# Transposes in place of identity and flip matmuls, GpSimd's list reordered, and normalisation parts three steps apart instead of four, in a hybrid decoder layer

## The chip, the cores and the metric

The kernel runs on one core of one Trainium2 chip. The metric is device time in microseconds (us) from start to end of the program; three runs of the kernel before are shown, and their median counts. The profile is of one execution, and its times count from the first instruction. TensorE multiplies, VectorE and ScalarE work element by element, GpSimd does the same more slowly without reaching PSUM, and SyncE only issues DMAs. Each engine works its own list in order; semaphores order the engines among one another.

## The reference, cut to what matters

One layer over 2,064 prompt positions (16 of them learned meta tokens) and 8 samples, in fp32. A combined projection gives, among others, the input of a convolution branch and queries, keys and values. The kernel's middle stage computes two things:

```
# convolution branch: 31 taps per channel, bias, LayerNorm over the 512 channels
y  = depthwise_causal_conv(u, w) + b
yn = (y - mean(y)) * rsqrt(mean((y - mean(y))**2) + 1e-5)   # then scale, shift, silu in the last stage
# attention branch, 8 heads, 2 key heads: masked softmax over the selected keys
p  = softmax(q @ k.T / 8 + bias, over the selected keys);  o = p @ v
```

The last stage multiplies both branches with their gates, projects them with `w_out`, adds the input and normalises.

## The kernel before, in words

The program is four stages with a barrier between them; the third, `attend_and_convolve`, is the one that changes, and the fourth, `mix_out`, reads what it writes (`d_y`, the normalised convolution, and `d_mix`, the gated attention).

**Steps.** Positions are cut into 17 tiles of 128, the last (16) with 16 prompt rows and the samples. Tiles go from 16 down to 0; each but the last has four pairs of heads, and one pair of one tile is a step p (`pairs`, 65 steps, step 0 for tile 16; tile i has steps 4(15-i)+1 to 4(15-i)+4). A tile of index i attends to (i+1) x 128 keys, so steps become shorter. In a step TensorE issues the scores of step p+1 (`logits`, lines 1710 and 1711, into psU), waits for the exponentials of step p, transposes them in groups (line 1717, into psT) and multiplies with the values (line 1733, into psO). VectorE adds mask and bias to the scores and takes the maximum (line 1606), ScalarE takes the exponential (line 1461) and copies the transposes to SBUF (line 1436, which is a helper, `evac`, for all copies out of psT). VectorE is about one step ahead of TensorE, as its work on step p+1 needs only TensorE's first part of step p.

**R.** After the fourth pair of a tile the reciprocal sums of the softmax, spread by VectorE to `rx` (line 1585), are turned into `rb` by four matmuls with the identity (line 1807); ScalarE copies them ahead of its next exponentials, and `finish` (VectorE) multiplies them into the output two steps later and signals `tile_done`.

**The convolution** runs in steps 2 to 16 (line 1746). Its normalisation is cut into nine parts k (`NORM`): tile 16 with the samples, and then two tiles each. Three lists give the step of each part's work (`SUM_STEP`, `SQ_STEP`, `TURN_STEP`). Part k goes: VectorE sums over channels in a partition (`sums`), TensorE sums over partitions (line 1752, job M), ScalarE copies the mean; two steps later VectorE subtracts it, GpSimd squares (`squares`, line 1409); at `SQ_STEP` VectorE sums the squares, TensorE sums over partitions (job V), ScalarE copies the variance; GpSimd takes its power -1/2 (`inverse_deviation`, lines 1415 and 1416); at `TURN_STEP` VectorE multiplies it in (`normalise`), and TensorE turns the part (`turn`, lines 1757 to 1763), four matmuls a tile against a matrix `flip` that reverses each run of 32 positions. ScalarE copies the result to `cT` in channel-major order (lines 1495 to 1501), and SyncE stores it one step later (line 1350).

**GpSimd's list** goes step by step: first `band_mask` for the tile whose turn it is (every fourth step, for the tile that begins three steps later), then the convolution's work. `band_mask` waits for `tile_done` of two tiles before and for the DMA of the mask (line 1298), converts the mask (line 1387) and adds the bias band of eight heads (line 1395).

**SyncE's list** goes by the same steps: in each, the stores of turned tiles first, then the store of a finished tile's `mix` and the loads of the tile two ahead (queries, gate, mask).

**psT** has two buffers, taken in the order of a list of jobs (`ptjobs`) which follows the same step numbers; a job waits until the job two before it has been copied.

Of the kernel before, what the change touches and what calls it, by code (L numbers as in the profile page):

```python
# [19 lines left out]
P = 128  # L20
NT = -(-LP // P)
LAST = NT - 1
# [3 lines left out]
CC = C // 128  # L26
# [28 lines left out]
def t5_bucket(rel):  # L55
# [10 lines left out]
                  flip=(529 + BANDX + LS, 128), avg=(529 + BANDX + LS + 128, 128))  # L66
# [4 lines left out]
WIN = 32  # L71
WROWS = 2 * WIN
WPT = P // WIN
NWP = WPT * LAST + 1
# [1044 lines left out]
CONV_STEP = [x for q in CONV_STEPS for x in q]  # L1119

NORM = [[LAST]] + [[i - 1, i] for i in range(LAST - 1, 0, -2)]
SUM_STEP = [18 + 4 * k for k in range(len(NORM))]
SQ_STEP = [s + 3 for s in SUM_STEP]
TURN_STEP = [s + 5 for s in SUM_STEP]

# [1 line left out]
def attend_and_convolve(nc, t, mem):  # L1127
# [38 lines left out]
    with ExitStack() as ctx:  # L1166
# [6 lines left out]
        yc = sb("yc", [128, NW, P])  # L1173
# [13 lines left out]
        rx = sb("rx", [128, GRP, 2, HD])  # L1187
# [21 lines left out]
        flip = sb("flip", [128, 2, 128])  # L1209
# [151 lines left out]
        @block.gpsimd  # L1361
        def _(pool):
            G = nc.gpsimd
            G.memset(q16[:, :, :].bitcast(f32), 0.0).then_inc(q16_zero, 1)
            G.memset(uw[:, NWP:NW, :], 0.0).then_inc(uw_zero, 1)
            G.memset(mix[:, 0], 0.0).then_inc(mix_zero, 1)
            load_pages(pool, range(hp), ptab, t.cache_v, "o s n d -> (o s) (n d)", vpage, vpp_in)
            steps = [0]

            def chained(ins):  # L1370

                steps[0] += 1
                ins.then_inc(pstep, 1)
                pool.wait_ge(pstep, steps[0])
            pool.wait_ge(band_in, 16)

            def band_mask(n):

                i = TILE_ORDER[n]
                s = n % 2  # L1380
                a, k = band0(i), width(i) - band0(i)
                j0 = a - (i - 1) * P
                if n >= 2:
                    pool.wait_ge(tile_done, n - 1)
                if i >= 2:
                    pool.wait_ge(m_in[s], masks_loaded(n))
                    chained(G.tensor_scalar(mask[:, s, 0:width(i)], mask[:, s, 0:width(i)], -NEG, NEG, ALU.mult, ALU.add))  # L1387
                else:
                    chained(G.memset(mask[:, s, 0:P], 0.0))
                    chained(G.tensor_copy(mask[:, s, i * P:(i + 1) * P], part(mem.cst, "causal")))  # L1390
                if n == 0:
                    pool.wait_ge(b16_in, 16 * NH)
                    G.tensor_tensor(out=bm[:, s, 0, 0:k], in0=band16[:, :], in1=mask[:, s, a:a + k], op=ALU.add).then_inc(bm_ready, 1)
                    return
                G.tensor_tensor(out=bm[:, s, :, 0:k], in0=band[:, :, j0:j0 + k],
                                in1=mask[:, s, a:a + k].unsqueeze(1).to_broadcast([128, NH, k]), op=ALU.add).then_inc(bm_ready, 1)
            def squares(k):

                n = norm_count(k)
                pool.wait_ge(sub_done, k + 1)  # L1400
                if k == 0:
                    G.memset(cT[:, 0], 0.0).then_inc(turn_zero, 1)
                else:
                    pool.wait_ge(s2_done, k)
                if NORM[k][0] == LAST:
                    to = y2[:, 0:n, :]
                else:
                    to = y2[:, 0:n, :].rearrange("p (w i) c -> p w i c", i=2)
                G.tensor_tensor(out=to, in0=norm_windows(k, yc), in1=norm_windows(k, yc), op=ALU.mult).then_inc(y2_done, 1)

            def inverse_deviation(k):

                n = norm_count(k)
                pool.wait_ge(act_pt, act_copies(("V", k)))
                chained(G.tensor_scalar(ve[:, 0:n], var[:, k % 2, 0:n], 1.0, LN_EPS, ALU.mult, ALU.add))
                G.tensor_tensor(out=rs[:, k % 2, 0:n], in0=ve[:, 0:n], in1=mhalf[:, 0:n], op=ALU.pow).then_inc(rs_done, 1)
            chained(G.memset(mhalf[:, :], -0.5))

            mask_step = [0, 0] + [first_step(n - 1) + 1 for n in range(2, NT)]
            for p in range(NP_):  # L1420
                for n in range(NT):
                    if mask_step[n] == p:
                        band_mask(n)
                for k in range(len(NORM)):
                    if SUM_STEP[k] + 2 == p:
                        squares(k)
                    if SQ_STEP[k] + 1 == p:
                        inverse_deviation(k)

        @block.scalar  # L1430
        def _(act):
            A = nc.scalar

            def evac(job, out, src):
                act.wait_ge(pe_pt, pt_no[job] + 1)
                A.activation(out, src, ACT.Copy).then_inc(act_pt, 1)  # L1436
# [27 lines left out]
            for p, (i, j) in enumerate(pairs):  # L1464
                for b, k in groups(p):
                    job = ("T", p, b, k)
                    n = t_no[job]
                    act.wait_ge(pe_pv, NS + 1 + max(0, n - 2))
                    m = sides(p) * k * P
                    evac(job, pts[:, n % 3, 0:m], PT[:, pt_no[job] % 2, 0:m])  # L1470
                if p and j == GRP - 1:
                    n = tile_no[i]
                    if n >= 2:
                        act.wait_ge(tile_done, n - 1)
                    evac(("R", p), rb[:, n % 2].rearrange("p c t -> p (c t)"), PT[:, pt_no["R", p] % 2, :])
                if p + 1 < NP_:
                    if j == GRP - 1 and tile_no[i] >= 1:
                        act.wait_ge(ri_ready, tile_no[i])
                    exps(p + 1)
                for k, tiles in enumerate(NORM):  # L1480
                    if SUM_STEP[k] == p:
                        evac(("M", k), mean[:, k % 2, 0:norm_count(k)], PT[:, pt_no["M", k] % 2, 0:norm_count(k)])
                for k, tiles in enumerate(NORM):
                    if SQ_STEP[k] == p:
                        evac(("V", k), var[:, k % 2, 0:norm_count(k)], PT[:, pt_no["V", k] % 2, 0:norm_count(k)])
                for k, tiles in enumerate(NORM):
                    if TURN_STEP[k] == p:
                        for i in tiles:
                            n, job = turned[i], ("Y", k, i)
                            pt = PT[:, pt_no[job] % 2]  # L1490
                            if n >= 2:
                                act.wait_ge(cT_out[n % 2], 16 * (n // 2))
                            if i == LAST:
                                act.wait_ge(turn_zero, 1)
                                act.wait_ge(pe_pt, pt_no[job] + 1)
                                A.activation(cT[:, n % 2, :, SROW:SROW + NS],
                                             pt[:, P:P + NS * CC].rearrange("p (s g) -> p g s", g=CC), ACT.Copy)
                                evac(job, cT[:, n % 2, :, 0:WIN], pt[:, 0:P].rearrange("p (g o) -> p g o", o=WIN))
                            else:
                                evac(job, cT[:, n % 2].rearrange("p g (w o) -> p w g o", o=WIN),  # L1500
                                     pt.rearrange("p (w g o) -> p w g o", g=CC, o=WIN))

        @block.vector
        def _(dve):
# [137 lines left out]
        def _(pe):  # L1642
# [111 lines left out]
            def turn(k, i):  # L1754
                pt = take_pt(("Y", k, i))
                if i == LAST:
                    T.matmul(pt[:, 0:P], yc[:, NWP - 1, :], flip[:, 0, :], start=True, stop=True)
                    for s in range(NS):
                        last = T.matmul(pt[:, P + s * CC:P + (s + 1) * CC], yc[:, NWP + s, :],
                                        flip[:, 0, 0::WIN], start=True, stop=True)  # L1760
                else:
                    for w in range(WPT):
                        last = T.matmul(pt[:, w * P:(w + 1) * P], yc[:, w * LAST + i, :], flip[:, 0, :], start=True, stop=True)
                last.then_inc(pe_pt, 1)
            logits(0)
            pe.wait_ge(s_norm, 1)
# [20 lines left out]
            for p, (i, j) in enumerate(pairs):  # L1787
# [14 lines left out]
                if p and j == GRP - 1:  # L1802
                    n = tile_no[i]
                    pe.wait_ge(ri_ready, n + 1)
                    pt = take_pt(("R", p))
                    for jj in range(GRP):
                        last = T.matmul(pt[:, jj * P:(jj + 1) * P],
                                        rx[:, jj].rearrange("p a d -> p (a d)"), ident, start=True, stop=True)
                    last.then_inc(pe_pt, 1)
                for e, (q, a, k) in enumerate(CONV_JOBS):  # L1810
                    if CONV_STEP[e] == p:
# [408 lines left out]
```

## Time and profile before

| | us |
|---|---|
| median of three runs | 1701.25 (1700.36 to 1712.43) |
| span of the profiled execution, first to last instruction | 1700.2 |
| median less span | 1.05 |
| attention stage (880 to 1480): TensorE / ScalarE / VectorE / GpSimd busy | 543 / 333 / 290 / 110 of 600 |

The rows further down come from the profile of that execution. Matmuls overlap in the pipeline, so the duration of one is longer than the distance to the next; weight loads have rows of their own (PEld). The number in square brackets behind a row is the engine's idle time before it, with the engine and line that ended it. The granted clock is 1.00 at 2.4 GHz and 0.50 at 1.2 GHz; in a window it is the mean.

### The profile page before, as it was taken

What the parts mean: (1) busy time and instruction counts of PE and PEld (TensorE: products, weight loads), DVE (VectorE), ACT (ScalarE), POOL (GpSimd) and SP (SyncE); (2) the same over time, 40 slices, a digit from 0 to 9 for tenths busy, and PEclk for the clock granted to TensorE, in tenths of its full rate; (3) what the DMA queues carried; (4) which work ended last, traced back from release to release, by engine and by line L of the source; (5) the groups of instructions that cost most, each with busy time, mean ns of one, the idle gap of its engine ahead of it and who ended that gap; (6) DMA issues with size and microseconds to landing.
All of it is one profiled execution on the core that took longest, in us unless ns stands there. A gap on an engine that the chain in (4) does not pass through costs nothing. (4 is left out here: it accounts for less than half of the span.)

```text
span 1700.2 us, 28238 instructions
## 1 busy us (share of the span) xinstructions
PE 1513.3 (89%) x10647; PEld 1292.1 (76%) x10647; DVE 1003.3 (59%) x2123; ACT 697.9 (41%) x1238; POOL 415.0 (24%) x270
## 2 busy tenths in 40 slices
PE   5688989989998789999799999999999887569998
PEld 5686979978998769999577777776767665348886
DVE  3342998878988879888443444445455555333222
ACT  4354513253112352232225545556556654344331
POOL 2111224431115803222221001112222233043220
PEclk9999999999999999999879999999999999779999
DMA  7742365221357602224561513511111112295542
GB/s 237 219 107 50 68 92 119 67 75 54 84 161 222 157 22 72 70 75 125 163 156 36 115 37 79 113 35 34 39 45 50 58 61 77 81 231 162 173 149 93
DMA packets 183355, 172.71 MB, mean 102 GB/s; under 512 B 58956, under 2 KB 155348, under 8 KB 182700
## 3 DMA queue, kind: packets, MB, share of 16 engines
q1 hardware_dynamic: 176572, 152.91, 33.7%
q10 hardware_dynamic: 6136, 16.95, 3.4%
q8 instruction: 84, 1.38, 0.3%
q0 software_dynamic: 512, 1.05, 0.2%
q14 instruction: 51, 0.42, 0.1%
HBM read 109.35 MB, written 58.19 MB: 99 GB/s over the span
## 5 line engine op out<-in xcount | busy, mean ns | idle before, releaser
L845 PE MATMUL psum<-xh,wh 128*128 128x384 f32 (+1 forms) x1040 | 345.4, 332 | 23.1 <-ACT hst L782 11.5
L845 PE MATMUL psum<-xl,wh 128*128 128x384 f32 (+1 forms) x1040 | 341.6, 329 | 0.0
L845 PE MATMUL psum<-xh,wl 128*128 128x384 f32 (+1 forms) x1040 | 341.6, 328 | 0.0
L1436 ACT ACTIVATE pts<-psT 128x512 f32<-128x512 f32 (+1 forms) x302 | 167.1, 572 | 255.1 <-PE psT L1717 232.2
L845 PEld LDWEIGHTS psum<-xh,wh 128*128 128x128 f32 x1040 | 197.6, 190 | 26.4 <-ACT hst L782 15.2
L1606 DVE CUSTOM_DVE_ANT_0 L<-psU,mask 128x512 f32<-128x512 f32 (+3 forms) x260 | 143.5, 592 | 114.6 <-PE psU L1711 113.3
L1733 PE MATMUL psO<-pts,vs 128*64 128x128 f32 x2176 | 180.3, 287 | 27.2 <-ACT pts L1436 27.2
L845 PEld LDWEIGHTS psum<-xl,wh 128*128 128x128 f32 x1040 | 197.8, 190 | 0.0
L845 PEld LDWEIGHTS psum<-xh,wl 128*128 128x128 f32 x1040 | 197.5, 190 | 0.0
L995 DVE TENSOR_SCALAR_CACHE_REDUCE hit<-scores,T 128x1792 bf16<-128x1792 f32 (+8 forms) x120 | 184.6, 1538 | 11.7 <-issue 0.9
L693 POOL TENSOR_TENSOR wl<-uw,wh 128x1024 fp32r<-128x1024 f32 x44 | 121.5, 2762 | 276.8 <-ACT wh L730 276.8
L1717 PE MATMUL psT<-cst,L 128*128 128x128 f32 x1105 | 170.4, 283 | 14.2 <-ACT L L1461 12.1
L1733 PEld LDWEIGHTS psO<-pts,vs 128*64 128x64 f32 x2176 | 113.2, 136 | 81.6 <-ACT pts L1436 56.5
L1461 ACT ACTIVATE L<-L,nm 128x1920 f32<-128x1920 f32 (+16 forms) x129 | 154.4, 1201 | 19.3 <-DVE nm L1611 18.9
L1717 PEld LDWEIGHTS psT<-cst,L 128*128 128x128 f32 x1105 | 119.3, 141 | 49.3 <-issue 20.9
L1710 PE MATMUL psU<-keys,qt 128*128 128x512 f32 (+3 forms) x320 | 128.7, 406 | 2.2 <-DVE mx L1606 1.2
L1387 POOL TENSOR_SCALAR mask<-mask 128x2064 bf16<-128x2064 bf16 (+14 forms) x15 | 18.8, 1255 | 416.8 <-DMA mask<-d_mask 416.7
L1711 PE MATMUL psU<-iqs,qt 128*128 128x512 f32 (+3 forms) x320 | 116.0, 373 | 0.0
L2095 PE MATMUL psO<-woh,fh 128*128 128x512 f32 x272 | 85.3, 395 | 27.6 <-POOL fl L1977 27.6
L2039 DVE TENSOR_TENSOR res<-psO,xr 128x1024 f32<-128x1024 f32 x17 | 20.8, 1225 | 125.5 <-PE psO L2095 125.5
L855 PE MATMUL psum<-keys,iqs 128*128 128x512 f32 (+4 forms) x172 | 70.0, 409 | 26.8 <-ACT uw L791 20.3
L791 ACT ACTIVATE uw<-psum 128x1024 f32<-128x1024 f32 (+6 forms) x100 | 76.8, 806 | 40.7 <-DVE scores L944 25.4
(269 smaller groups left out, 2507.5 us busy)
## 6 DMA issues: line engine op xcount, KB each, us to landing
uw<-in_w_in SPq DMA_DIRECT2D x28, 512.0 KB
uw<-in_w_in SPq DMA_DIRECT2D x32, 256.0 KB
qt<-d_q SPq DMA_DIRECT2D x16, 512.0 KB, 4.0
xst<-in_x_prompt SPq DMA_DIRECT2D x15, 512.0 KB, 4.0
xr<-in_x_prompt SPq DMA_DIRECT2D x15, 512.0 KB, 4.4
out_y_prompt<-fin SPq DMA_DIRECT2D x15, 512.0 KB, 3.0
gate<-d_ga SPq DMA_DIRECT2D x17, 256.0 KB, 4.4
d_mix<-mix SPq DMA_DIRECT2D x17, 256.0 KB, 2.2
```

The source lines that it names most:

```text
L693: nc.gpsimd.tensor_tensor(out=wl[:, n % 2], in0=wst[:, n % 2], in1=wh[:, n % 2].bitcast(f32), op=ALU.subtract).then_inc(w_lo, 1)
L791: nc.scalar.activation(r[:, m % 2, 0:job[4]], u[:, 0:job[4]], ACT.Relu).then_inc(act_job, 1)
L845: last = nc.tensor.matmul(u[:, 0:k * P], a[:, w % 2, cc, :], x[:, s0:s0 + k, cc, :], start=(cc == 0 and e == 0), stop=(cc == KC - 1 and e ...
L995: V.tensor_scalar(hit[:, 0:width(i)], sc[c], at[:, c:c + 1] if len(at.shape) == 2 else at[:, c], 0.0, ALU.is_ge, ALU.add, accum_out=into[: ...
L1436: A.activation(out, src, ACT.Copy).then_inc(act_pt, 1)
L1461: A.activation(L[:, b, 0:width(i)], L[:, b, 0:width(i)], ACT.Exp, bias=nm[:, b:b + 1], accum_out=es[:, tile_no[i] % 2, j % GRP + 4 * side: ...
L1606: last = V.tensor_tensor_reduce(out=L[:, b, x0:x1], in0=u[:, x0 - a:x1 - a], in1=in1, scale=1.0, scalar=3 * NEG, op0=ALU.add, op1=ALU.max, ...
L1710: T.matmul(u[:, 0:k], q, kh[:, side, a:a + k], start=True, stop=False)
L1711: T.matmul(u[:, 0:k], q, kl[:, side, a:a + k], start=False, stop=True).then_inc(pe_u, 1)
L1717: last = T.transpose(pt[:, (side * k + e) * P:(side * k + e + 1) * P], L[:, (2 * p + side) % 4, (b + e) * P:(b + e + 1) * P], ident)
L1733: last = T.matmul(OT[64 * side:64 * side + 64, tile_no[i] % 2, j * P:(j + 1) * P], vs[0:rows, b + e, 64 * side:64 * side + 64], pts[0:rows ...
L2095: last = T.matmul(O[:, s, h * 512:(h + 1) * 512], a[:, n % FS, c, :], b[:, c, h * 512:(h + 1) * 512], start=(c == W_ORDER[0] and e == 0), ...
```

## The change

Four edits. R and the turns call the transpose, with the identity as the moving operand, in place of a matmul (with the identity for R and with `flip` for the turns; the samples' small matmuls of tile 16 stay). What `flip` reversed is now reversed in ScalarE's copy, which reads each run of 32 backwards. GpSimd's list has the convolution's work ahead of the mask in a step, and the inverse deviation ahead of the squares. And parts follow one another every three steps: `SUM_STEP` goes 18, 21, ..., 42 in place of 18, 22, ..., 50; `SQ_STEP` and `TURN_STEP` stay 3 and 5 steps behind it. So turns come at steps 23, 26, ..., 47 in place of 23, 27, ..., 55.

```
-SUM_STEP = [18 + 4 * k for k in range(len(NORM))]
+SUM_STEP = [18 + 3 * k for k in range(len(NORM))]
...
             for p in range(NP_):
+                for k in range(len(NORM)):
+                    if SQ_STEP[k] + 1 == p:
+                        inverse_deviation(k)
+                    if SUM_STEP[k] + 2 == p:
+                        squares(k)
                 for n in range(NT):
                     if mask_step[n] == p:
                         band_mask(n)
-                for k in range(len(NORM)):
-                    if SUM_STEP[k] + 2 == p:
-                        squares(k)
-                    if SQ_STEP[k] + 1 == p:
-                        inverse_deviation(k)
...
-        evac(job, cT[:, n % 2, :, 0:WIN], pt[:, 0:P].rearrange("p (g o) -> p g o", o=WIN))
+        evac(job, cT[:, n % 2, :, 0:WIN], pt[:, 0:P].rearrange("p (g o) -> p g o", o=WIN)[:, :, ::-1])
...
-             pt.rearrange("p (w g o) -> p w g o", g=CC, o=WIN))
+             pt.rearrange("p (w g o) -> p w g o", g=CC, o=WIN)[:, :, :, ::-1])
...
-                    T.matmul(pt[:, 0:P], yc[:, NWP - 1, :], flip[:, 0, :], start=True, stop=True)
+                    T.transpose(pt[:, 0:P], yc[:, NWP - 1, :], ident)
...
-                        last = T.matmul(pt[:, w * P:(w + 1) * P], yc[:, w * LAST + i, :], flip[:, 0, :], start=True, stop=True)
+                        last = T.transpose(pt[:, w * P:(w + 1) * P], yc[:, w * LAST + i, :], ident)
...
-                        last = T.matmul(pt[:, jj * P:(jj + 1) * P],
-                                        rx[:, jj].rearrange("p a d -> p (a d)"), ident, start=True, stop=True)
+                        last = T.transpose(pt[:, jj * P:(jj + 1) * P], rx[:, jj].rearrange("p a d -> p (a d)"), ident)
```

## Rows read from the trace of the kernel before

**Rows 1.** Head of the page: span of the profiled execution.
```profile
span 1700.2 us, 28238 instructions
```

**Rows 2.** Windows, attention stage: length, busy time by engine, granted clock, DMA share, GB/s.
```profile
880.00:1480.00 600.00, 543.35 (x5301) 407.73 (x5299) 289.77 (x1051) 333.34 (x601) 110.16 (x60) 0.98 0.22 59
```

**Rows 3.** Timeline of weight loads: start, length, engine, line, operation, count.
```profile
1225.30 0.90 PEld L1717 LDWEIGHTS psT<-cst,L 128*128 128x128 f32 x8
...
1241.02 1.86 PEld L1763 LDWEIGHTS psT<-flip,yc 128*128 128x128 f32 x16 [0.17 <-issue]
1242.80 0.19 PEld L1710 LDWEIGHTS psU<-keys,qt 128*128 128x128 f32 x1
...
1251.72 0.97 PEld L1807 LDWEIGHTS psT<-cst,rx 128*128 128x128 f32 x8 [0.17 <-issue]
1252.61 0.19 PEld L1710 LDWEIGHTS psU<-keys,qt 128*128 128x128 f32 x1
```

**Rows 4.** Groups, 880 to 1480: count, busy, mean ns, idle before and releaser.
```profile
L1717 PE MATMUL psT<-cst,L 128*128 128x128 f32 x1099 | 169.8, 283 | 14.2 <-ACT L L1461 12.1 <-ACT uw L1436 2.1
...
L1763 PE MATMUL psT<-flip,yc 128*128 128x128 f32 x128 | 19.7, 317 | 10.0 <-DVE yc L1507 10.0
...
L1807 PE MATMUL psT<-cst,rx 128*128 128x128 f32 x128 | 19.5, 297 | 0.0
...
L1507 DVE TENSOR_TENSOR yc<-yc,rs 128x1024 f32<-128x1024 f32 (+1 forms) x9 | 11.2, 1240 | 55.0 <-POOL rs L1416 55.0
```

**Rows 5.** Timeline of GpSimd around the deviation of part 7.
```profile
1417.62 0.51 POOL L1387 TENSOR_SCALAR mask<-mask 128x384 bf16<-128x384 bf16 x1 [13.03 <-DMA mask<-d_mask]
1418.21 4.07 POOL L1395 TENSOR_TENSOR bm<-band,mask 128x2048 f32<-128x2048 f32 x1
1422.36 0.20 POOL L1415 TENSOR_SCALAR ve<-var 128x8 f32<-128x8 f32 x1
1422.65 1.65 POOL L1416 TENSOR_TENSOR rs<-ve,mhalf 128x8 f32<-128x8 f32 x1
```

**Rows 6.** Timeline of VectorE (parts 1 and 7) and ScalarE (variance of part 7).
```profile
1231.91 1.23 DVE L1507 TENSOR_TENSOR yc<-yc,rs 128x1024 f32<-128x1024 f32 x1 [4.50 <-POOL rs L1416]
...
1424.33 1.22 DVE L1507 TENSOR_TENSOR yc<-yc,rs 128x1024 f32<-128x1024 f32 x1 [8.52 <-POOL rs L1416]
...
1413.40 0.17 ACT L1436 ACTIVATE var<-psT 128x8 f32<-128x8 f32 x1
```

**Rows 7.** Timeline of TensorE: where it stood behind VectorE's lateness, and a statistic.
```profile
1273.58 0.50 PE L1710 MATMUL psU<-keys,qt 128*128 128x512 f32 x1 [1.24 <-DVE mx L1606]
...
1347.81 1.07 PE L1717 MATMUL psT<-cst,L 128*128 128x128 f32 x8 [1.03 <-ACT uw L1436]
...
1375.80 1.07 PE L1717 MATMUL psT<-cst,L 128*128 128x128 f32 x8 [0.67 <-ACT uw L1436]
...
1399.23 3.57 PE L1763 MATMUL psT<-flip,yc 128*128 128x128 f32 x16 [2.66 <-DVE yc L1507]
...
1416.41 0.39 PE L1752 MATMUL psT<-s,flip 128*128 128x8 f32 x2
...
1425.61 3.78 PE L1763 MATMUL psT<-flip,yc 128*128 128x128 f32 x16 [5.45 <-DVE yc L1507]
...
1448.66 0.85 PE L1717 MATMUL psT<-cst,L 128*128 128x128 f32 x6 [0.40 <-ACT uw L1436]
```

**Rows 8.** Windows, TensorE's steps 46, 47, 50 and 51.
```profile
1386.85:1391.80 4.95, 4.64 (x43) 3.54 (x42) 2.21 (x14) 3.16 (x10) 0.62 (x1) 1.00 0.65 191
1391.80:1402.46 10.66, 7.69 (x57) 6.50 (x56) 4.32 (x16) 4.35 (x13) 5.94 (x3) 0.86 0.01 2
1412.99:1416.66 3.67, 3.36 (x33) 2.66 (x32) 2.27 (x11) 2.55 (x8) 0.00 (x0) 1.00 0.97 305
1416.66:1429.05 12.39, 6.63 (x47) 5.86 (x46) 4.05 (x12) 3.78 (x10) 6.84 (x5) 0.77 0.01 4
```

**Rows 9.** Timeline of SyncE's queue: the mask's DMA issue.
```profile
1413.53 0.50 SPq L1298 DMA_DIRECT2D mask<-d_mask  x1
```

**Rows 10.** Timeline of ScalarE: copies of a pair of turned tiles, and the next copy.
```profile
1242.97 1.07 ACT L1436 ACTIVATE uw<-psT 128x512 f32<-128x512 f32 x2
1246.15 1.09 ACT L1436 ACTIVATE pts<-psT 128x512 f32<-128x512 f32 x2 [2.11 <-PE psT L1717]
```

## The prediction

> **What bounds the kernel now.** I read the busy shares first, then the stretch that the change touches, then the waits inside it. The profiled execution spans 1700.2 us [rows 1]; the median of the three timed runs, 1701.25, is 1.05 us above it, so a saving worked out on this trace is taken off 1701.25. All edits lie in the attention stage, 880 to 1480 us. There TensorE has matmuls in flight for 543 of 600 us, VectorE is busy 290, ScalarE 333, GpSimd 110 [rows 2]. The next stage starts behind a barrier, so what this stage gains reaches the end one to one. A step p of TensorE is: scores of step p+1, transposes and products of step p, then the extras (R, statistics, turns). In wide tiles its order has hardly a gap; in narrow ones, from about 1340 us on, there are real stalls, and those are what I price beside the cheaper instructions.
>
> **Transposes for matmuls.** A 128x128 fp32 matmul is two load-and-multiply records here: 16 R groups of four matmuls leave 128 records, 16 turned tiles of four leave 128 [rows 4]. One R takes the weight port from 1251.72 to the next score load at 1252.61, 0.89 us; a pair of turns from 1241.02 to 1242.80, 1.78 us; eight transposes are one record each and take 0.90 us with a tail of 0.14, so (0.90 - 0.14) / 7 = 0.109 us each [rows 3]. R falls to 4 x 0.109 = 0.44 and saves 0.45, sixteen times: 7.2 us. A pair of turns falls to 0.87 and saves 0.91, eight times: 7.3, and the last tile's single matmul 0.1. Is it on the path? Behind R, ScalarE must copy R before it can do the next exponentials, and TensorE's transposes wait for those; an earlier R moves that whole chain. Behind a turn TensorE goes straight on to scores; ScalarE's two copies end 2.11 us before it gets its next tile [rows 10]. So both count in full: 14.6 us. The Trainium skill's page "TensorE: Matmul & The Clock Gate", section Terms, calls the transpose mode four times faster for fp32; that would make a transpose 0.056 us and this term 21.5 us, a time of about 1666. The row is of this very form of instruction, so I keep 0.109.
>
> **The reversal moves into ScalarE's copy,** which reads PSUM backwards inside each run of 32. No row shows a backward read. Bounds: nothing, or a doubling of 0.53 us per copy [rows 10], 8.5 us over 16 copies if none is hidden. A pair has 2.11 - 0.91 = 1.2 us of slack against 1.07, so I take nothing and keep half of the upper end, 4.3 us, for narrow tiles in the range.
>
> **GpSimd's order.** GpSimd runs one list. At a step where a mask is due it now waits for the mask's DMA, does mask and bias sum, and only then the inverse deviation. In the last full case the variance is copied at 1413.40, but GpSimd takes up the mask at 1417.62 and starts the deviation's two instructions at 1422.36 [rows 5, 6]. VectorE wants it at 1424.33 - 8.52 = 1415.81 and stands 8.52 us; in the wide tile of the other row it stands 4.50 [rows 6]. Behind it stand the next scores' evacuations, and the turn of that part, on TensorE. With the convolution's work first, the two instructions (0.20 and 1.65 us) run right behind the variance: ready at about 1415.6, just as VectorE arrives.
>
> What this wait costs on the path: TensorE stands before turns for 10.0 us in all [rows 4], of which 2.66 and 5.45 in the two worst places, and 1.24 once for score banks [rows 7]: 11.2. VectorE's lateness is felt once more in the step behind, at 1347.81, 1375.80 and 1448.66: 1.03 + 0.67 + 0.40 = 2.1 [rows 7]. And in both worst places the granted clock falls while TensorE stands: a mean of 0.86 and 0.77 in steps 47 and 51 [rows 8], so for a part of them at 1.2 rather than 2.4 GHz. Step 47 takes 10.66 us; its neighbour without a turn 4.95, with 0.25 for a statistic (1416.41 to 1416.66) [rows 7]. 10.66 - 4.95 + 0.25 - 1.78 - 2.66 = 1.5 us are the clock's. Step 51: 12.39 - 3.67 + 0.25 - 1.78 - 5.45 = 1.7. Together 3.2, and all of it goes: 16.5 us for the stalls.
>
> **Three steps apart.** Turns come at steps 23, 26, ..., 47 rather than 23, 27, ..., 55, so they leave the narrowest tiles, where VectorE had least cover. Amounts are unchanged. What now meets: (a) the mean of part k+1 and the variance of part k in one step: two copies of 0.17 us [rows 6] instead of one before the next transposes, hidden except behind R. (b) Normalise and subtract the mean in one VectorE step: 1.2 us more there; TensorE's step is longer than VectorE's list by that, so nothing. (c) R and a turn both at steps 32 and 44: the turn runs in the gap in which TensorE waits for exponentials anyway, worth up to 0.9 us each, a small gain I leave out. (d) SyncE's queue: at steps 30 and 42 the stores of a turned tile now stand ahead of the next tile's loads, and they wait for ScalarE's copies. That holds the loads 4 to 6 us; a mask is issued at 1413.53 and used at 1417.62 [rows 5, 9], so it lands 4 us after issue, and GpSimd, in order, holds the inverse deviation behind it. VectorE then stands 3 to 5 us at turns 3 and 7. Waits of that size cost between 0 and 1.24 now [rows 6, 7]; I take 1 each. (e) The mask of the tile at step 53: its bias sum ends at 1418.21 + 4.07 = 1422.28 [rows 5]. The steps ahead shrink to 3.67 - 0.25 = 3.42 us [rows 8], and VectorE could come at 1412.99 - 0.25 + 2 x 3.42 = 1419.6: the mask is up to 2.7 late. That step follows an R, where TensorE waits for ScalarE anyway; 0 to 2.7, I take 1. GpSimd's squares now ahead of the mask wait for VectorE inside the same step, shorter than the mask's DMA; the mask has two steps to spare elsewhere: nothing.
>
> **Sum:** 14.6 + 16.5 - 3 = 28 us, so 1701.25 - 28 = 1673.
>
> **Rivals.**
> A. The wait is moved, not removed: the mask ahead in GpSimd's list, or SyncE's queue, holds the deviation at most turns as now. For it: the list stays one list, and collisions (d) exist. Against: a mask falls due every 4 steps and a deviation every 3, so they can meet at one in four, and there the deviation now goes first. Then only 14.6 is left: 1687.
> B. The transposes save no time, since the path runs through ScalarE or they too take two records. Against: existing transposes are single records [rows 3]. The stalls alone, less 3: 1701.25 - 13.5 = 1688.
> C. Slower: the clock. At each of 24 places (16 R, 8 pairs of turns) matmuls become transposes; if each place sent the granted clock down once, at the 1.5 to 1.7 us of [rows 8], that is 36 to 41 us against a gain of 28: 1709 to 1714. It decides from some 19 places on. For it: both falls in [rows 8] come in narrow steps with little work on TensorE, and turns become shorter. Against: transposes are in every step of the stage, 1,099 of them, and its mean granted clock is 0.98 [rows 2, 4]. The same page, Part 4, says that the full clock does not engage for transposes. The trace so far does not bear that rule out.
>
> **Chances.** Forecast 0.72, with its own range: at best 14.6 + 16.5, the 1.8 of (c), the 0.5 of hidden statistics and no new cost, 33.4, so 1668; at worst all new costs (3, with 1.7 more for (e)), 4.3 for the copies and two new falls of the clock at 1.5, so 31.1 - 12.0 = 19.1, 1682. A 0.15, B 0.08, C 0.05. The whole range, 1666 (a transpose cheaper than its row) to 1688, takes in A and B. About 1% is what a measurement of this kernel can tell from no change, 1684.2 to 1718.3. Faster: the forecast and the lower third of A, 0.77; same: the rest of A and B and most of C, 0.20; slower 0.03, the part of C in which a fall costs more than priced.
>
> **What would show it.** R and turn records: 64 each instead of 128, at about 0.11 us. VectorE's wait for the inverse deviation: from 55.0 us over nine [rows 4] to under 20, largest at turns 3 and 7. TensorE's wait before turns: near 0, with full clock from step 23 to the last tiles. Copies of turned tiles at 0.53 us each. The stage ends near 1452 instead of 1480. I am wrong if VectorE's nine waits stay above 4 us each (A), if scores after an R start no earlier (B), or if steps with turns show a granted clock of one half (C).

## The result and the profile after

The changed kernel takes 1676.38 us (median of 4 runs, 1674.21 to 1678.09) against 1702.2 us for the kernel before (4 runs): 25.8 us saved by the medians. The ratio over all runs is 0.9834, 95% interval 0.9809 to 0.9858 (one run of the kernel before took 1712.43 us, which the median leaves aside). Timed again later, with the experiments, the ratio was 0.9852 [0.9836, 0.9867]. Forecast were 1673 us and a range of 1666 to 1688. The profiled execution spans 1676.4 us against 1700.2 [rows 1].

The saving lies in the attention stage. From its first score matmul to the next stage's first load it took 607.2 us before and takes 582.5 now, 24.7 less. The first view is the windows over it, over four of TensorE's steps (44, 52, 53 and 54), over two stretches inside them, and over the stage up to step 43 and its last 11 us: length, busy time of PE, PEld, DVE, ACT and POOL, granted clock, DMA share, GB/s.

```profile
880.00:1456.00 576.00, 526.58 (x5175) 389.75 (x5172) 298.24 (x1053) 332.01 (x601) 111.86 (x60) 0.98 0.23 62
...
1362.07:1374.65 12.58, 7.61 (x59) 6.08 (x57) 6.14 (x19) 4.29 (x11) 5.96 (x4) 0.80 0.00 1
1407.45:1412.71 5.26, 3.46 (x34) 2.74 (x33) 2.05 (x12) 1.85 (x5) 2.45 (x1) 1.00 0.00 0
1412.71:1418.23 5.52, 3.97 (x25) 2.92 (x23) 2.88 (x12) 3.84 (x11) 1.40 (x3) 0.62 0.14 50
1418.23:1422.29 4.06, 3.65 (x24) 3.07 (x23) 1.52 (x10) 1.46 (x5) 3.17 (x1) 0.68 0.65 194
...
1369.70:1376.50 6.80, 4.49 (x18) 3.91 (x19) 3.38 (x14) 3.19 (x7) 0.97 (x1) 0.50 0.00 1
1414.00:1420.80 6.80, 5.59 (x28) 4.72 (x28) 3.66 (x19) 2.90 (x10) 3.97 (x3) 0.50 0.46 145
...
880.00:1369.00 489.00, 463.06 (x4685) 342.02 (x4682) 255.12 (x844) 284.90 (x474) 91.84 (x48) 1.00 0.23 61
1444.80:1456.00 11.20, 5.31 (x24) 3.05 (x24) 3.02 (x13) 2.94 (x12) 0.00 (x0) 0.50 0.10 41
```

The stage ends at 1456, forecast 1452, and TensorE's busy time is 17 us lower than in [rows 2]. The mean clock, 0.98, hides what the single steps show: step 44 took 12.58 us at a mean of 0.80 (7.11 before), and steps 53 and 54 ran at 0.62 and 0.68 (5.52 and 4.06 us against 4.63 and 2.94 before). The next two windows are the two falls themselves: 6.8 us each at 0.50, the lower of the clock's two levels, 1.2 GHz. Up to step 43 the clock stays at 1.00; in the last 11 us it is at 0.50. The kernel before has two such stretches beside the falls of [rows 8], one right behind the turn of tile 16, at 1201, and one at its own end:

```profile
1201.60:1204.80 3.20, 3.20 (x11) 2.62 (x10) 2.75 (x10) 0.00 (x1) 0.00 (x0) 0.50 0.27 82
...
1467.80:1480.00 12.20, 6.79 (x31) 4.23 (x30) 3.66 (x16) 3.27 (x12) 0.00 (x0) 0.50 0.11 41
```

The end aside, the half clock lasts 13.7 us in either kernel: three falls of 3.4, 3.4 and 6.8 us before, two of 6.8 us now. Stalls are not gone; a few are left, in new places.

The groups of the same stretch, which answer to [rows 4]: out<-in, shape, count, then busy time, mean ns of one, and the idle time before them with what ended it.

```profile
L1717 PE MATMUL psT<-cst,L 128*128 128x128 f32 x1102 | 171.0, 284 | 8.2 <-ACT L L1461 7.8 <-ACT uw L1436 0.3
...
L1507 DVE TENSOR_TENSOR yc<-yc,rs 128x1024 f32<-128x1024 f32 (+1 forms) x9 | 12.2, 1358 | 11.3 <-POOL rs L1416 11.0
...
L1807 PE MATMUL psT<-cst,rx 128*128 128x128 f32 x64 | 11.4, 305 | 6.0 <-DVE rx L1585 6.0
...
L1763 PE MATMUL psT<-cst,yc 128*128 128x128 f32 x64 | 9.9, 298 | 0.3 <-ACT rb L1436 0.3
...
L1436 ACT ACTIVATE uw<-psT 128x512 f32<-128x512 f32 (+1 forms) x17 | 8.8, 568 | 0.0
```

R and turns are 64 records each instead of 128. VectorE's nine waits for the inverse deviation came from 55.0 us to 11.3, TensorE's waits before turns from 10.0 to 0.3. New is 6.0 us in front of R, where nothing was waited for before. The copies that now read backwards take 568 ns on average (566 before).

The weight port at a pair of turns, which answers to [rows 3] (start, length, count):

```profile
1228.72 0.86 PEld L1763 LDWEIGHTS psT<-cst,yc 128*128 128x128 f32 x8 [0.17 <-issue]
1229.54 0.19 PEld L1710 LDWEIGHTS psU<-keys,qt 128*128 128x128 f32 x1
```

1229.54 - 1228.72 = 0.82 us, where the pair took 1.78. Where VectorE still waits for the deviation, from its timeline, which answers to [rows 6]:

```profile
1182.49 1.99 DVE L1507 TENSOR_TENSOR yc<-yc,rs 128x1152 f32<-128x1152 f32 x1
1184.40 5.11 DVE L1507 TENSOR_TENSOR yc<-yc,mean 128x1024 f32<-128x1024 f32 x1
...
1276.05 1.23 DVE L1507 TENSOR_TENSOR yc<-yc,rs 128x1024 f32<-128x1024 f32 x1 [4.70 <-POOL rs L1416]
...
1366.34 1.22 DVE L1507 TENSOR_TENSOR yc<-yc,rs 128x1024 f32<-128x1024 f32 x1 [6.33 <-POOL rs L1416]
...
1409.93 0.29 DVE L1606 CUSTOM_DVE_ANT_0 L<-psU,mask 128x128 f32<-128x128 f32 x1 [3.32 <-POOL bm L1395]
```

The two waits are at parts 3 and 7, the parts of item (d). Part 7 is followed back through GpSimd's list (which answers to [rows 5]) and SyncE's queue (which answers to [rows 9]):

```profile
1183.36 5.07 POOL L1395 TENSOR_TENSOR bm<-band,mask 128x2048 f32<-128x2048 f32 x1
...
1359.38 0.73 POOL L1387 TENSOR_SCALAR mask<-mask 128x640 bf16<-128x640 bf16 x1 [14.64 <-DMA mask<-d_mask]
1360.20 4.09 POOL L1395 TENSOR_TENSOR bm<-band,mask 128x2048 f32<-128x2048 f32 x1
1364.37 0.20 POOL L1415 TENSOR_SCALAR ve<-var 128x8 f32<-128x8 f32 x1
1364.65 1.65 POOL L1416 TENSOR_TENSOR rs<-ve,mhalf 128x8 f32<-128x8 f32 x1
```

```profile
1351.62 0.91 SPq L1350 DMA_DIRECT2D d_y<-uw  x2
1352.58 0.55 SPq L1354 DMA_DIRECT2D d_mix<-mix  x1
1354.57 0.68 SPq L1298 DMA_DIRECT2D mask<-d_mask  x1
```

The mask is issued behind the turned tiles' stores, at 1354.57. GpSimd stands 14.64 us for it, does mask and bias sum, and only then the two instructions of the deviation. What that costs on TensorE (second row), with two other places that the account below comes back to:

```profile
1190.18 0.50 PE L1710 MATMUL psU<-keys,qt 128*128 128x512 f32 x1 [1.10 <-DVE mx L1606]
...
1372.02 1.12 PE L1807 MATMUL psT<-cst,rx 128*128 128x128 f32 x4 [4.50 <-DVE rx L1585]
...
1412.30 0.66 PE L1807 MATMUL psT<-cst,rx 128*128 128x128 f32 x4 [1.49 <-DVE rx L1585]
```

At 1372.02 R of step 44 stands 4.50 us for `rx`, since VectorE made it behind its 6.33 us wait; R itself then takes 1.12 us rather than 0.66 us, because the granted clock had fallen to half (from 1369.7 on). That is the form of [rows 8], in another step.

### The profile page after: what moved, and what is told of

The parts are those of the page before. It is cut to its first block and busy times, and to the rows that moved or that the text cites. A ratio compares the mean times of both kernels' runs of the same rounds, so it can differ in the third digit from the quotient of the medians.

```text
span 1676.4 us, 27980 instructions
## 1 busy us (share of the span) xinstructions
PE 1498.1 (89%) x10518; PEld 1275.7 (76%) x10518; DVE 1011.1 (60%) x2123; ACT 696.3 (42%) x1238; POOL 417.8 (25%) x270
## 3 DMA queue, kind: packets, MB, share of 16 engines
q8 instruction: 83, 1.36, 0.3%
```

## The experiments

Every ratio below is against the kernel before on the same chip.

**One edit at a time.** Each of the first three is the kernel before with one edit; the fourth is the changed kernel with two blocks of SyncE's loop exchanged.

*Transposes and reversed copy alone.* The changed kernel, with

```
-SUM_STEP = [18 + 3 * k for k in range(len(NORM))]
+SUM_STEP = [18 + 4 * k for k in range(len(NORM))]
...
+                for n in range(NT):
+                    if mask_step[n] == p:
+                        band_mask(n)
                 for k in range(len(NORM)):
-                    if SQ_STEP[k] + 1 == p:
-                        inverse_deviation(k)
                     if SUM_STEP[k] + 2 == p:
                         squares(k)
-                for n in range(NT):
-                    if mask_step[n] == p:
-                        band_mask(n)
+                    if SQ_STEP[k] + 1 == p:
+                        inverse_deviation(k)
```

> The kernel before with the transposes and the reversed copy alone (parts four steps apart, mask ahead in GpSimd's list). My theory, TensorE's issue time is on the path: 16 R at 0.45 to 0.50 us and 8 pairs of turns at 0.87 to 0.91, 14.2 to 15.3 us less than before, some 1687. Rival B, the time is hidden behind ScalarE's chain: within 3 us of before. Rival C, the clock pays for it: new windows at half clock behind R or turns, and less than 10 us gained. GpSimd and VectorE should show the same nine waits for the inverse deviation, 50 to 58 us in all.

Measured: 1698.27 us, ratio 0.9969 [0.9959, 0.9978], 5 us, where 14 to 15 were expected. VectorE's group, and TensorE's turns of parts 6 and 7:

```profile
L1507 DVE TENSOR_TENSOR yc<-yc,rs 128x1024 f32<-128x1024 f32 (+1 forms) x9 | 11.2, 1241 | 53.7 <-POOL rs L1416 53.7
```

```profile
1392.82 1.97 PE L1763 MATMUL psT<-cst,yc 128*128 128x128 f32 x8 [2.46 <-DVE yc L1507]
...
1419.79 1.97 PE L1763 MATMUL psT<-cst,yc 128*128 128x128 f32 x8 [6.49 <-DVE yc L1507]
```

VectorE waits as long as before. TensorE reaches the turn of part 7 earlier and stands 6.49 us there instead of 5.45 [rows 7]: part of what the transposes save becomes a longer stand. The fall of the clock at part 6 lasts 6.8 us instead of 3.4, and one of 3.4 us, from 1429.5, is new. In its profiled execution the stage is 10.5 us shorter; that execution, 1692.94 us, was the shortest of ten, so the median's 5 is the surer figure.

*GpSimd's order alone.* The kernel before, with

```
-                for n in range(NT):
-                    if mask_step[n] == p:
-                        band_mask(n)
                 for k in range(len(NORM)):
+                    if SQ_STEP[k] + 1 == p:
+                        inverse_deviation(k)
                     if SUM_STEP[k] + 2 == p:
                         squares(k)
-                    if SQ_STEP[k] + 1 == p:
-                        inverse_deviation(k)
+                for n in range(NT):
+                    if mask_step[n] == p:
+                        band_mask(n)
```

> The kernel before with GpSimd's new list order alone (matmuls kept, four steps apart). My theory, the mask ahead of the inverse deviation makes all nine waits: VectorE's 55 us fall to under 10, TensorE's waits before turns to near 0, both falls of the clock at 1399 and 1423 us go; 14 to 16.5 us less than before, some 1686. In addition, normalise now runs under GpSimd's bias sum and should take longer than its 1.23 us, as the subtraction did in the changed kernel (5.1 us in two places). Rival, the waits come from the variance arriving late: waits stay above 4 us each and the time within 3 us of before.

Measured: 1685.2 us, ratio 0.9909 [0.9896, 0.9922]: 17.9 us by the medians, 15.5 by the ratio. In the profiled execution, the shortest of five, the stage is 18.1 us shorter. Its groups, and the window from the end of its one early fall of the clock (1201 to 1204.8, as before) on:

```profile
L1763 PE MATMUL psT<-flip,yc 128*128 128x128 f32 x128 | 16.4, 281 | 0.0
...
L1507 DVE TENSOR_TENSOR yc<-yc,rs 128x1024 f32<-128x1024 f32 (+1 forms) x9 | 13.2, 1471 | 0.0
...
1204.80:1450.20 245.40, 217.15 (x1880) 165.97 (x1878) 144.56 (x515) 149.40 (x316) 74.78 (x43) 1.00 0.20 63
```

Both waits are zero, and the two falls of [rows 8] are gone. The normalisation is held by the bias sum by less than 1 us each time (2.15 us at most), not by 4; one subtraction takes 4.24 us. Order of one engine's list, not one instruction fewer, gives most of the change.

*Three steps alone.*

```
-SUM_STEP = [18 + 4 * k for k in range(len(NORM))]
+SUM_STEP = [18 + 3 * k for k in range(len(NORM))]
```

> The kernel before with three steps between parts alone (matmuls kept, mask ahead in the list). My theory, parts 0, 4 and 8 still meet a mask in the same step and wait 4 to 8 us each, parts 3 and 7 wait behind a mask that SyncE's queue delays, and the mask of step 53 comes late; of the 16.5 us of stalls some 10 to 13 are replaced: 2 to 7 us less than before. Rival, three steps apart is itself what removes the stalls, because turns leave the narrow tiles: 12 us or more less than before.

Measured: 1706.94 us, ratio 1.0018 [1.0003, 1.0034]: slightly slower, where a gain was expected. Its groups:

```profile
L1807 PE MATMUL psT<-cst,rx 128*128 128x128 f32 x128 | 21.3, 317 | 5.6 <-DVE rx L1585 5.6
...
L1507 DVE TENSOR_TENSOR yc<-yc,rs 128x1024 f32<-128x1024 f32 (+1 forms) x9 | 11.2, 1240 | 28.0 <-POOL rs L1416 27.8
...
L1763 PE MATMUL psT<-flip,yc 128*128 128x128 f32 x128 | 19.7, 318 | 4.0 <-DVE yc L1507 4.0
```

The waits halve, since masks and deviations meet less often, but the worst now meet an R. TensorE's stands before turns and R (4.0 + 5.6) are as much as before (10.0). That is rival A's mechanism, in a kernel that keeps the old order.

*Loads ahead of stores.* The changed kernel; in SyncE's loop over steps the block below is moved behind the store of `d_mix` and the next tile's loads:

```
                 for k, tiles in enumerate(NORM):
                     if p == TURN_STEP[k] + 1:
...
                             sp.wait_ge(act_pt, act_copies(("Y", k, i)))
                             sp.dma_start(t.d_y...)
```

> The changed kernel with one block moved: in SyncE's list the finished tile's store and the next tile's loads come ahead of the stores of turned tiles in the same step. My theory, the stores at steps 30 and 42 hold the mask's load and with it the inverse deviation of parts 3 and 7: VectorE's waits of 4.7 and 6.3 us fall below 1, TensorE's stand of 4.5 us before R in step 44 goes with the fall of the clock behind it; 5 to 6.5 us less than the changed kernel's 1676.4, some 1670.5. Rival, the variance's copy or GpSimd's own work makes these two waits: no change. Step 52's late mask (1.5 us and a fall of the clock) should stay.

Measured: 1672.44 us, ratio 0.9823 [0.98, 0.9846]. The group of the deviation, TensorE's R of step 44, the window of that step, and SyncE's issue of the mask:

```profile
L1507 DVE TENSOR_TENSOR yc<-yc,rs 128x1024 f32<-128x1024 f32 (+1 forms) x9 | 12.0, 1334 | 0.9 <-POOL rs L1416 0.7
```

```profile
1369.43 0.65 PE L1807 MATMUL psT<-cst,rx 128*128 128x128 f32 x4
```

```profile
1364.06:1371.25 7.19, 6.41 (x59) 5.02 (x57) 4.78 (x18) 3.94 (x9) 1.89 (x1) 1.00 0.00 1
```

```profile
1351.30 0.50 SPq L1298 DMA_DIRECT2D mask<-d_mask  x1
```

The mask is issued at 1351.30, 3.27 us sooner; the waits of parts 3 and 7 go (11.3 to 0.9 us), R of step 44 stands for nothing, the clock does not fall there, and step 44 takes 7.19 us instead of 12.58. So SyncE's queue made that stall, and it cost 5.4 us in its step. The late mask of step 52 and a fall of the clock behind it (3.4 us) stay, as expected. In the timed runs the intervals of this kernel and of the changed one overlap: the trace shows the cause, the timing alone does not prove the gain.

**The order undone.** To see whether the order carries the change inside it too: the changed kernel with the mask ahead again (second half of the first diff above, alone).

> The changed kernel with the mask ahead again in GpSimd's list (transposes and three steps kept). My theory, the list order carries most of the gain and the transposes pay fully only where no turn stands for the deviation: with three steps and the old order the waits of parts 0, 3, 4, 7 and 8 are back, as with three steps alone, so 6 to 12 us less than before, 1691 to 1697. Rival, transposes and three steps together do without the order: 1680 or less.

Measured: 1693.19 us, ratio 0.993 [0.9907, 0.9953], as expected. Groups:

```profile
L1507 DVE TENSOR_TENSOR yc<-yc,rs 128x1024 f32<-128x1024 f32 (+1 forms) x9 | 11.2, 1239 | 31.6 <-POOL rs L1416 31.4
...
L1763 PE MATMUL psT<-cst,yc 128*128 128x128 f32 x64 | 10.8, 317 | 4.9 <-DVE yc L1507 4.6 <-ACT rb L1436 0.3
```

Some 14 to 17 us are lost with the order (against the changed kernel's two timings, 1679.27 and 1676.38), nearly what it gave alone.

**What three steps cost.** The changed kernel with four steps kept (`18 + 4 * k`), beside the changed kernel as it is, on one chip:

> The changed kernel with parts four steps apart again (transposes, reversed copy and GpSimd's new order kept). The list order alone took 15.5 us off, three steps apart alone added 3; transposes alone took only 5 off, because where a turn stood for the deviation the time saved turned into a longer stand. My theory: with the stalls gone the transposes are worth their 14 to 15 us, and four steps apart has no collision of stores with loads: 1668 to 1673, 4 to 9 us less than the changed kernel on the same chip. Rival, turns in narrow tiles cost what the three steps save: the changed kernel's time or more.

> The changed kernel itself, for comparison on the same chip: a ratio of 0.981 to 0.986 to the kernel before.

Measured: four steps 1673.56 us, 0.9821 [0.9806, 0.9836]; the changed kernel 1679.27 us, 0.9852 [0.9836, 0.9867]. The intervals only touch: on this chip moving the turns closer costs some 5.7 us. Against the changed kernel's first timing (0.9834) the difference is 2 us and the intervals overlap, so the size is less sure than the sign, for which the stalls of the trace speak too. The kernel with four steps is the better one here, and no other version run here is clearly better than it. Its stage takes 576.8 us, 30.4 less than before. One long stall is left in it, in step 52, where R stands 2.55 us; VectorE's and GpSimd's timelines there:

```profile
1400.37 5.06 DVE L1507 TENSOR_TENSOR yc<-yc,mean 128x1024 f32<-128x1024 f32 x1
```

```profile
1400.25 4.09 POOL L1395 TENSOR_TENSOR bm<-band,mask 128x2048 f32<-128x2048 f32 x1
```

The same subtraction takes 1.2 us elsewhere. It began 0.12 us behind GpSimd's bias sum and ended 1.09 us after it: behind it come VectorE's next scores, and only then the copy of `rx`, for which R stands. That GpSimd held VectorE is so far read from the times alone; the next runs move the bias sum, and then cut it.

**The bias sum moved.** In two kernels (on top of loads ahead of stores with three steps, and with four) a mask is loaded as soon as VectorE has taken the last scores that need its buffer, and GpSimd takes it one step sooner, ahead of the convolution's work:

```
-            mask_step = [0, 0] + [first_step(n - 1) + 1 for n in range(2, NT)]
+            mask_step = [0, 0] + [first_step(n - 1) for n in range(2, NT)]
...
+                sp.wait_ge(nm_ready, sides_before(last_step(n - 2) + 1))
                 sp.dma_start(mask[:, s, 0:width(i)], t.d_mask[i, :, 0:width(i)]).then_inc(m_in[s], 16)
```

> The kernel of the run with loads ahead of stores, and the mask two steps earlier: SyncE loads a tile's mask as soon as VectorE has taken the last scores of the tile two before (not when that tile is finished), and GpSimd does mask and bias sum one step earlier in its list, ahead of the convolution's work. My theory: the bias sum no longer lies under the subtraction (steps 23 and 35: 5.1 us back to 1.2), and the mask of step 53 is in time (VectorE's wait of 3.3 us, TensorE's 1.5 us before R and the fall of the clock behind it go): 3 to 5 us less than with the loads ahead alone, 1667 to 1669. Rival, the subtraction is slow for another reason (two long operations in a row): it stays at 5.1 us.

> As the run with the mask early, but parts four steps apart. The bias sum then lies in a step where VectorE has neither a normalisation nor a subtraction: all 18 of these should take 1.2 to 1.4 us, and GpSimd's bias sum 4.1. My theory: 1 to 3 us less than four steps kept without it. Rival: no difference, as what VectorE loses there is hidden.

Measured: with three steps 1672.54 us, 0.982 [0.9798, 0.9842], no better than loads ahead of stores alone, though 3 to 5 us less were expected. With four 1679.51 us, 0.9856 [0.984, 0.9872], slower than the kernel with four steps that it was to mend. The latter's VectorE, GpSimd and TensorE:

```profile
1404.45 4.15 DVE L1595 COPY rx<-ri 128x512 f32<-128x512 f32 x1
```

```profile
1404.26 4.06 POOL L1405 TENSOR_TENSOR bm<-band,mask 128x2048 f32<-128x2048 f32 x1
```

```profile
1408.66 0.66 PE L1817 MATMUL psT<-cst,rx 128*128 128x128 f32 x4 [3.58 <-DVE rx L1595]
```

The subtractions are back to 1.21 to 1.35 us as expected, but now the copy that makes `rx`, 0.43 us where nothing holds it, runs into the bias sum, and R stands 3.58 us for it. With three steps it is the normalisation (5.10 us at 1342.57) and `rx` (3.49 us at 1367.67). In these two kernels the collision moved on to the next instruction of VectorE with two inputs in SBUF, or from SBUF to SBUF.

**The bias sum split.** The kernel with four steps, its bias sum in four instructions of two heads each; and the same with the mask loaded early and taken first in the list, at its old step:

```
-                G.tensor_tensor(out=bm[:, s, :, 0:k], in0=band[:, :, j0:j0 + k], ...)
+                for h in range(0, NH, 2):
+                    last = G.tensor_tensor(out=bm[:, s, h:h + 2, 0:k], in0=band[:, h:h + 2, j0:j0 + k], ...)
```

> Four steps kept, with GpSimd's bias sum as four instructions of two heads in place of one of eight. Seen so far: VectorE's normalisation, subtraction and rx copy stand for as long as one bias sum of 4.1 us runs, and then take 1.2. My theory, the engines exclude each other for the length of one instruction: with pieces of some 1.0 us none of VectorE's 18 normalisations and subtractions takes over 2.5 us, the sum in all takes 4.2 to 6 us, and TensorE's stand of 2.55 us before R in step 52 shrinks or stays if the mask is late instead; 0 to 4 us less than four steps kept. Rival, GpSimd's pieces run back to back and VectorE is still held for the whole 4 us: no change.

> As the sum split, with the mask loaded early (as soon as VectorE has taken the last scores of the tile two before) and taken first in GpSimd's list in the step where it stood. My theory: no VectorE operation is held over 2.5 us and no mask is late; TensorE's stand before R in step 52 falls below 0.5 us and the fall of the clock behind it goes: 4 to 8 us less than four steps kept on the same chip, 1666 to 1669. Rival, narrow tiles have another bound there: within 2 us of four steps kept.

Measured: 1676.72 us, 0.9843 [0.9822, 0.9863], and 1677.81 us, 0.985 [0.9834, 0.9866]. GpSimd and VectorE of the first:

```profile
1395.67 5.49 POOL L1396 TENSOR_TENSOR bm<-band,mask 128x512 f32<-128x512 f32 x4
```

```profile
1395.78 2.13 DVE L1509 TENSOR_TENSOR yc<-yc,mean 128x1024 f32<-128x1024 f32 x1
...
1401.20 0.29 DVE L1608 CUSTOM_DVE_ANT_0 L<-psU,mask 128x128 f32<-128x128 f32 x1 [3.29 <-POOL bm L1396]
```

The hold is now about one piece long (2.13 instead of 5.06 us), which bears the cause out, and with the early mask R of step 52 stands 0.45 us. Yet neither is faster than the kernel with four steps, where up to 4 and 4 to 8 us less were expected. In the first R still stands 2.97 us in step 52: VectorE waits 3.29 us for the bias sum, which is late. In the second the clock falls for 6.8 us, behind TensorE's waits of 1.25 and 0.75 us only:

```profile
1423.40:1430.20 6.80, 5.85 (x32) 4.38 (x28) 2.19 (x12) 2.35 (x10) 0.00 (x0) 0.50 0.50 154
```

The changed kernel has the same two waits at 1430.49 and 1431.89 and no fall there. And the fall of the kernel before at 1201 came behind no wait over 0.31 us, but behind 16 small matmuls for the samples, which the changed kernel has too, without a fall. What sets off the falls is not settled by these runs.

## Why the prediction was right, by its steps

| term | forecast, us | by the stage of one profiled execution, us | by the timed ratios, us |
|---|---|---|---|
| transposes, stalls gone | 14.6 | 12.3 (order alone 589.1, with both 576.8) | 15.0 (0.9909 to 0.9821) |
| stalls of GpSimd's order | 16.5 | 18.1 (before 607.2, order alone 589.1) | 15.5 (1 to 0.9909) |
| three steps | -3 | -5.7 (576.8, changed 582.5) | -5.3 (0.9821 to 0.9852) |
| sum | 28 | 24.7 | 25.2 |

The last column takes the ratios times 1703 us; each carries some 2 to 3 us of interval, so the first two terms are met within that, and the third is the one furthest off for its size.

**The order of the list was read right, place and size.** The prediction took the 55.0 us of VectorE's waits as harmless where TensorE had other work and counted only the stands, their knock-on and the half clock. With the order alone these went. In the changed kernel the half clock is back, at other places, for as long as before, so full clock "from step 23 to the last tiles" is the one sign that did not come. Rival A, the wait moved, is out in the changed kernel: 11.3 us is left, at two parts, not at most turns. It is what three steps with the old order do (28.0 us left and no gain).

**Transposes: right as a row, not as something that counts in full by itself.** One record each, at the price of its row. Their 14.6 us were said to lie on the path in both places. They do once TensorE does not stand before turns; alone they gave 5. The prediction added the two terms as if each held without the other. It did no harm here because both edits came together, which is luck of the combination: nothing in the prediction worked out that the first term hangs on the second. Rival B is out: R steps became 0.50 us shorter (step 16: 14.93 to 14.42) and pairs of turns 0.96 on the weight port. On the Trainium skill, page "TensorE: Matmul & The Clock Gate", section Terms: by its factor of four the time would have been 1666. The trace does not agree: the pair's eight loads take the weight port 0.82 us against 1.78, a factor of about two.

**The reversal costs nothing,** as taken: 568 ns a copy against 566 before.

**Item (d) was foreseen at its place and priced too low.** SyncE's stores ahead of the loads did hold the mask (3.27 us between the two kernels, 4 to 6 forecast), and VectorE stood 4.70 and 6.33 us at parts 3 and 7 (3 to 5 forecast). The price of 1 us each came from waits in the trace before that had cost 0 to 1.24. At part 3, a wide tile, TensorE shows no stand for it, and the clock stays at full. At part 7 the list runs into an R: VectorE's lateness became a 4.50 us stand before R and a fall of the clock, 5.4 us in that step. The prediction looked for the turn that would wait, not for the R of the same step; (c), the meeting of R and turn in steps 32 and 44, was put down as a small gain, and at step 44 it is where the loss is.

**Item (e), the late mask of step 53,** was forecast up to 2.7 us late and taken at 1. VectorE waits 3.32 us for the bias sum at 1409.93, R of step 52 stands 1.49, and steps 53 and 54 run 0.9 and 1.1 us longer at a lower clock: some 3.5 us in all.

**Item (b) was priced at nothing and is not nothing.** Normalising and subtracting in one step was to cost VectorE 1.2 us under TensorE's cover. But the subtraction runs under GpSimd's bias sum and takes 5.1 us, not 1.22, in steps 23 and 35. In step 23 TensorE stands 1.10 us for score banks, and that step takes 12.87 us against 11.34 with four steps; step 35 shows no loss (7.89 against 7.88). Nothing in the trace of before set those two instructions beside each other: all 18 normalisations and subtractions take 1.21 to 1.36 us there.

So the term that was mis-sized is the price of three steps: 3 us forecast, 5 to 6 measured on one chip, because a meeting was priced by the wait it makes on VectorE and not by the R behind it. The items sum to more than that. The kernel with four steps has a stall of its own in step 52, and closer turns may give something back in the narrow tiles, which was not measured by itself.

**Rival C is out.** Ten of the 16 R and six of the eight pairs of turns lie ahead of 1369 us, and up to there the clock stays at 1.00. The two falls behind came with and after stands of TensorE (4.50 and 1.49 us). The Trainium skill, page "TensorE: Matmul & The Clock Gate", Part 4, by which the full clock does not engage for transposes, is not borne out here: 1,102 transposes of exponentials [rows 4 show 1,099] run in a stage at 0.98. They stand among other matmuls, so what transposes by themselves would do to the clock no run here shows.

## What to carry to other kernels

An in-order list is read for what waits for a transfer ahead of what is ready: putting the short ready instructions first gave 16 to 18 us with not one instruction fewer, and made another edit, worth 5 us alone, worth 12 to 15. When something is moved to other steps, list for every engine and queue what it newly meets in each step, the group that waits behind it included, and price a meeting by the work that follows in that step, not by the cheapest wait seen elsewhere. Here the spacing of three, the one part that changed no amount of work, took back a fifth of the gain on the chip where both were timed.

## What was not expected of the hardware

While GpSimd adds two arrays in SBUF (the bias sum, 4.06 to 4.14 us), instructions of VectorE that read two arrays in SBUF, or copy from SBUF to SBUF, hardly move: the subtraction takes up to 5.13 us instead of 1.2, the copy of `rx` up to 4.15 instead of 0.43, and they end about 1.1 us behind the bias sum or sooner. It holds the other way too: where the normalisation was running already (1182.49 in the timeline of VectorE above), the bias sum that started 0.9 us later took 5.07 us. VectorE's instructions on scores in PSUM show no such hold: one of 512 columns takes 0.69 us under a bias sum as elsewhere. The Trainium skill, page "GPSIMD Engine Reference", section 1, says that the two engines share their way to SBUF and contend when VectorE's instruction has two SBUF inputs; the trace agrees for the subtraction and the normalisation. By these rows the one that is first holds the other for about the length of a whole instruction, since cutting the sum in four cut the hold from 5.06 to 2.13 us.
